# RWKV-7 mixer: the 32x32 diagonal blocks of the chunk matrices inverted column by column on VectorE

## What is computed

```python
def rwkv7_step(state, inp):
    r_t, w_t, k_t, v_t, a_t, b_t = inp
    sa = jnp.einsum('bhvk,bhk->bhv', state, a_t)
    state = (state * w_t[:, :, None, :] + sa[..., None] * b_t[:, :, None, :]
             + v_t[..., None] * k_t[:, :, None, :])
    return state, jnp.einsum('bhvk,bhk->bhv', state, r_t)
```

## Time and profile before

| what | us |
|---|---|
| median of 3 runs | 2700.04 |
| lowest and highest of them | 2699.19, 2700.79 |
| the profiled execution's own time | 2704.08 |
| its span (first to last instruction) | 2700.3 |
| busy in the span: TensorE / VectorE / ScalarE / GpSimd | 2652.0 / 2121.3 / 1292.1 / 109.4 |
| the mixer's stage from the first value product to the end of chunk 1's outputs | 803.9 to 982.0 |

### The profile page before, as it was taken

The page is one execution under the profiler, slowest core; times in us unless marked ns, Lnnn a source line. Parts: engine busy times, 40 slices in busy tenths (PEclk is TensorE's granted clock), DMA queues, the critical chain, the costliest instruction groups (busy, mean ns, idle before and its releaser), DMA issues.

```text
span 2700.3 us, 51095 instructions
## 1 busy us (share of the span) xinstructions
PE 2652.0 (98%) x20514; PEld 2458.9 (91%) x20514; DVE 2121.3 (79%) x3219; ACT 1292.1 (48%) x1780; POOL 109.4 (4%) x109
## 2 busy tenths in 40 slices
PE   8999999999999999999999999999999999999999
PEld 7998799999888989999879999986899999859999
DVE  7986589899765647995987878499878887987877
ACT  5345553443532324335565544555554464564543
POOL 0000000000013310000000000000000000000000
PEclk9999999999999999999999999999999999999999
DMA  7764267667431015764424455431345544404454
GB/s 273 280 233 157 94 258 279 238 253 280 155 140 63 1 73 219 280 233 172 157 79 156 166 185 183 168 141 63 110 156 187 188 156 155 153 19 145 168 186 155
DMA packets 61229, 456.22 MB, mean 169 GB/s; under 512 B 6840, under 2 KB 6864, under 8 KB 8736
## 3 DMA queue, kind: packets, MB, share of 16 engines
q1 hardware_dynamic: 54432, 395.86, 40.1%
q0 software_dynamic: 6656, 58.35, 5.4%
HBM read 453.12 MB, written 1.07 MB: 168 GB/s over the span
## 4 chain that ended last, share of the span: by engine, by line
PE 88%; DVE 5%; ACT 3%; DMA 3%; issue 1%; DVEq 0%; SPq 0%; ACTq 0%
PE ps L777 22%; PE ps L616 14%; PE ps L617 14%; PE ps L618 14%; PE ps L1058 3%; DMA ring<-in_weights 3%; PE ps L1452 3%; PE ps L1459 1%; ACT arena L2087 1%; PE ps L1311 1%; PE ps L1148 1%; PE ps L1141 1%; PE ps L558 1%; PE ps L1294 1%; DVE w_parts L2158 1%
## 5 line engine op out<-in xcount | busy, mean ns | idle before, releaser
L1624 ACT ACTIVATE w_parts<-ring 128x1024 fp32r<-128x1024 f32 x462 | 463.4, 1052 | 402.3 <-PE ps L616 284.9
L616 PE MATMUL ps<-normed_parts,w_parts 128*128 128x256 f32 x2160 | 602.3, 279 | 1.7 <-DVE w_parts L2158 1.7
L617 PE MATMUL ps<-normed_parts,w_parts 128*128 128x256 f32 x2160 | 603.7, 279 | 0.0
L618 PE MATMUL ps<-normed_parts,w_parts 128*128 128x256 f32 x2160 | 603.0, 279 | 0.0
L2158 DVE SCALAR_TENSOR_TENSOR w_parts<-ring,w_parts 128x1024 fp32r<-128x1024 f32 x462 | 544.6, 1220 | 50.0 <-ACT w_parts L1624 49.4
L777 PE MATMUL ps<-stream_high,half_parts 128*128 128x256 f32 x2224 | 422.8, 286 | 2.5 <-DVE half_parts L2363 1.6
L616 PEld LDWEIGHTS ps<-normed_parts,w_parts 128*128 128x128 f32 x2160 | 406.0, 188 | 2.3 <-DVE w_parts L2158 2.3
L618 PEld LDWEIGHTS ps<-normed_parts,w_parts 128*128 128x128 f32 x2160 | 406.0, 188 | 0.0
L617 PEld LDWEIGHTS ps<-normed_parts,w_parts 128*128 128x128 f32 x2160 | 405.9, 188 | 0.0
L2363 DVE SCALAR_TENSOR_TENSOR half_parts<-ring,half_parts 128x1024 fp32r<-128x1024 f32 x225 | 271.9, 1213 | 130.3 <-ACT half_parts L1711 129.4
L777 PEld LDWEIGHTS ps<-stream_high,half_parts 128*128 128x128 f32 x2224 | 347.9, 188 | 7.6 <-issue 5.6
(11 more groups left out here) (459 smaller groups left out, 4197.2 us busy)
## 6 DMA issues: line engine op xcount, KB each, us to landing
ring<-in_weights SPq DMA_DIRECT2D x374, 1024.0 KB, 4.8
arena<-in_mod_weights POOLq DMA_DIRECT2D x32, 1536.0 KB, 8.2
arena<-in_cond POOLq DMA_DIRECT2D x8, 512.0 KB, 6.6
arena<-toeplitz_rows POOLq DMA_DIRECT2D x1, 1536.0 KB, 12.3
x<-in_x SPq DMA_DIRECT2D x1, 1024.0 KB, 4.7
arena<-in_ctx POOLq DMA_DIRECT2D x1, 1024.0 KB, 5.4
out<-x SPq DMA_DIRECT2D x1, 1024.0 KB, 3.9
const<-in_const SPq DMA_DIRECT2D x1, 999.0 KB, 11.4
```

Of the source, the lines that this page charges most:

```text
L616: first = pe.matmul(into, wh, high, start=start, stop=False, skip_group_check=True)
L617: pe.matmul(into, wh, low, start=False, stop=False, skip_group_check=True)
L618: return first, pe.matmul(into, wl, high, start=False, stop=stop, skip_group_check=True)
L1624: a(w_parts[:, to, 0, cols], ring[:, at, cols], ACT.Copy).then_inc(s["w_high"], 1)
```

## The change

Levels 0 to 4, by which blocks of 32 come to be, are taken out of the doubling. In their place each of the 4 diagonal 32x32 blocks of each of the 32 matrices is inverted by itself, all 128 at once, one on each partition of VectorE. The steps are:

- TensorE multiplies `rw_b` with `AR_a` for all 16 heads of a chunk, in one group of 16 matmuls of 128 columns each (`diagonal(c)`), for both chunks ahead of the values; these are the same numbers as the first half of `products`, which are still made later.
- ScalarE keeps the diagonal blocks alone, in four copies on 32 partitions each (`keep_diagonal`), into `small_in`.
- VectorE masks them, transposes by blocks of 32 so that each partition holds one 32x32 block, sets the diagonal to 1, and runs 30 columns of elimination, each one a product and a sum of (31 - j) x j elements, each waiting for the one before. Two transposes bring the inverses back (`small_n`, `small_t`).
- `Tn` and `Tt` are set to zero beforehand, for chunk 0 by VectorE and for chunk 1 by GpSimd, and ScalarE puts the blocks in place, in eight copies on 32 partitions a chunk (`spread_small`).
- The level of n = 32 and the last one stay. GpSimd masks once for a group, with `next_t`, instead of five times.
- `narrow(5)` stands ahead of the values and its weight tile ahead of theirs in the stream. The four products of chunk 0 stand behind all values. The copies of the turned keys and b go from VectorE to ScalarE.
- The table of constants has `next_t` and `small_above` instead of `below`, `level0`, `level0_t` and `levels_t`.

The core of the diff:

```diff
-CONSTANTS = [("ident", P), ("ones", P), ("head_ones", P), ("below", P), ("upto", P), ("above", P), ("level0", P),
-             ("level0_t", P), ("levels_t", 6 * P), ("flip", P), ("head_columns", 62), ("both_rows", 16)]
+SMALL = 32
+CONSTANTS = [("ident", P), ("ones", P), ("head_ones", P), ("upto", P), ("above", P), ("next_t", P), ("flip", P),
+             ("small_above", SMALL), ("head_columns", 62), ("both_rows", 16)]
...
+    n = SMALL
+    put("next_t", ((i[:, None] // (2 * n) == i[None] // (2 * n)) & (i[None] // n % 2 == 1) & (i[:, None] // n % 2 == 0)).astype(np.float32))
+    put("small_above", (i[:, None] % n < np.arange(n)[None]).astype(np.float32))
...
+        Tn_all, Tt_all = carve(16384, 4 * NB, P), carve(18432, 4 * NB, P)
+
+        MATRICES = NT * RW_HEADS
+        small_in = carve(0, MATRICES, SMALL)
+        small_x, small_step = carve(22528, SMALL, SMALL), carve(23552, SMALL * SMALL // 4)
+        small_n, small_t = carve(0, MATRICES, SMALL), carve(1024, MATRICES, SMALL)
...
+                if c:
+                    pool.wait_ge(s["rw_u"], 2 * c)
+                    nc.gpsimd.memset(Tn_all, 0.0)
+                    nc.gpsimd.memset(Tt_all, 0.0).then_inc(s["small_zero"], 1)
+                    pool.wait_ge(s["top_C"], 6 * c)
+                for b in range(NB):
+                    pool.wait_ge(s["rwA_copied"], NB * c + b + 1)
+                    nc.gpsimd.tensor_tensor(Am[b], At[b], C("next_t").unsqueeze(1).broadcast_to((P, 4, P)), ALU.mult).then_inc(s["am_ready"], 1)
...
-                    pe.wait_ge(s["rw_r_out"], p + 1)
+                    pe.wait_ge(*((s["rw_r_out"], p + 2) if p < 3 else (s["mm_evac"], mm0 + 16)))
...
+                def diagonal(c):
+
+                    for b in range(NB):
+                        for p in in_turn:
+                            m, half = heads[b][p]
+                            bank, at = 4 + 2 * half + b // 2, (2 * (b % 2) + p % 2) * P
+                            mm = pe.matmul(ps[:, bank, at:at + P], rw_b[rows[half], m, c * P:(c + 1) * P], AR[rows[half], m, c, 0], start=True, stop=True)
+                    mm.then_inc(s["rw_side"], 1)
+
+                pe.wait_ge(s["rw_ab"], 4)
+                diagonal(0)
+                narrow(5, (P, P), free=(s["rw_r_out"], 1))
+                pe.wait_ge(s["diag_kept"], 1)
+                diagonal(1)
                 value(0)
+                value(1)
                 pe.wait_ge(s["rw_rk"], 1)
+                pe.wait_ge(s["diag_kept"], 2)
                 for p in range(4):
...
-                mm.then_inc(s["rw_bs"], 1)
-                value(1)
+                mm.then_inc(s["rw_side"], 1)
+                value(2)
...
-                mm.then_inc(s["rw_turn"], 1)
-                value(2)
+                mm.then_inc(s["rw_side"], 1)
+                value(3)
                 pe.wait_ge(s["rw_turned"], 2)
                 products(0, 0)
-                value(3)
-                products(0, 1)
                 pe.wait_ge(s["mm_evac"], mm_n[0])
...
-                mm.then_inc(s["rw_turn"], 1)
+                mm.then_inc(s["rw_side"], 1)
+                products(0, 1)
                 products(0, 2)
+                products(0, 3)
                 pe.wait_ge(s["rw_v_turned"], 1)
 
-                narrow(5, (P, P))
-                products(0, 3)
-
                 def invert(c):
 
-                    with pe.Fori(0, 4) as l:
-                        for step in ("B0", "B1", "C0", "B2", "C1", "B3", "C2", "C3"):
-                            b = int(step[1])
-                            if step[0] == "B":
-                                pe.wait_ge(s["inv_T"], 20 * c + 4 * l + b + 1)
-                                pe.wait_ge(s["am_ready"], 20 * c + 4 * l + b + 1)
...
+                    pe.wait_ge(s["small_spread"], c + 1)
                     for step in ("B0", "B1", "C0", "B2", "B3", "C1", "C2", "C3"):
                         b = int(step[1])
                         if step[0] == "B":
-                            pe.wait_ge(s["inv_T"], 20 * c + 16 + b + 1)
-                            pe.wait_ge(s["am_ready"], 20 * c + 16 + b + 1)
+                            pe.wait_ge(s["am_ready"], NB * c + b + 1)
...
+                            if b == 0:
+                                pe.wait_ge(s["rwA_copied"], NB * (c + 1))
+                                pe.wait_ge(s["rwA_masked"], 2 * NB * (c + 1))
...
+                def keep_diagonal(c):
+
+                    actv.wait_ge(s["rw_side"], c + 1)
+                    for r in small_rows:
+                        by_half = ps[r, 4:8, :].rearrange("q (h d) (e n t) -> q h (d e) n t", h=2, e=2, n=2)[:, :, :, :, r]
+                        ins = a(small_in[r, of_chunk(c), :].rearrange("q (b h n) t -> q h b n t", h=2, n=2), by_half, ACT.Copy)
+                    ins.then_inc(s["diag_kept"], 1)
+
...
+                def spread_small(c, whole, small, which):
+
+                    for r in [small_rows[i] for i in which]:
+                        ins = a(whole[r, :, r], small[r, of_chunk(c), :], ACT.Copy)
+                    return ins
...
+                keep_diagonal(0)
+                evac(g_lora[:, 0, :], ACT.Sigmoid, m=0, last=False)
+                evac(g_lora[:, 1, :], ACT.Sigmoid, m=1, incs=2)
+                keep_diagonal(1)
+                value(0, 2)
+                value(1, 2)
+                actv.wait_ge(s["rw_side"], 3)
...
+                value(2, 2)
+                actv.wait_ge(s["rw_side"], 4)
+                for i, dst in enumerate((k_tok, b_tok)):
+                    a(dst, ps[:, 4 + 2 * i:6 + 2 * i, :].rearrange("p b t -> p (b t)"), ACT.Copy).then_inc(s["rw_turned"], 1)
+                value(3, 1)
...
                 strict(0)
-                value(3)
+                actv.wait_ge(s["rw_side"], 5)
+                a(rw_v, ps[:, 0:4, :].rearrange("p (c b) t -> p c (b t)", c=NT), ACT.Copy).then_inc(s["rw_v_turned"], 1)
+                actv.wait_ge(s["small_done"], 1)
                 strict(1)
-                actv.wait_ge(s["rw_turn"], 2)
-                a(rw_v, ps[:, 0:4, :].rearrange("p (c b) t -> p c (b t)", c=NT), ACT.Copy).then_inc(s["rw_v_turned"], 1)
+                spread_small(0, Tn_all, small_n, (0, 1))
...
                 strict(2)
-                evac(g_lora[:, 0, :], ACT.Sigmoid, m=0, last=False)
-                evac(g_lora[:, 1, :], ACT.Sigmoid, m=1)
+                spread_small(0, Tn_all, small_n, (2, 3))
                 strict(3)
+                spread_small(0, Tt_all, small_t, (0, 1, 2, 3)).then_inc(s["small_spread"], 1)
...
-                    with actv.Fori(0, 4) as l:
-                        for b in range(NB):
-                            actv.wait_ge(s["inv_B"], 16 * c + 4 * l + b + 1)
-                            a(Bs[b].rearrange("p n t -> p (n t)"), ps[:, b, :], ACT.Copy).then_inc(s["inv_Bs"], 1)
...
+                actv.wait_ge(s["small_zero"], 1)
+                spread_small(1, Tn_all, small_n, (0, 1, 2, 3))
+                spread_small(1, Tt_all, small_t, (0, 1, 2, 3)).then_inc(s["small_spread"], 1)
...
-                dve.wait_ge(s["rw_turn"], 1)
-                for i, dst in enumerate((k_tok, b_tok)):
-                    nc.vector.tensor_copy(dst, ps[:, 4 + 2 * i:6 + 2 * i, :].rearrange("p b t -> p (b t)")).then_inc(s["rw_turned"], 1)
+                link.mark(nc.vector.memset(Tn_all, 0.0))
+                link.mark(nc.vector.memset(Tt_all, 0.0))
+
+                def small_inverses():
+
+                    in_turn = lambda v: v.rearrange("p h t -> p t h")
+                    mask = C("small_above", SMALL).unsqueeze(1).broadcast_to((P, MATRICES, SMALL))
+                    dve.wait_ge(s["diag_kept"], 2)
+                    link(tt(small_in, small_in, mask, ALU.mult))
+                    link(nc.vector.transpose(small_x, in_turn(small_in)))
+                    link.mark(nc.vector.memset(flat(small_x)[:, 0:SMALL * SMALL:SMALL + 1], 1.0))
+                    for j in range(1, SMALL - 1):
+                        n = SMALL - 1 - j
+                        below = small_x[:, j + 1:SMALL, 0:j]
+                        step = small_step[:, 0:n * j].rearrange("p (i k) -> p i k", i=n)
+                        link(tt(step, small_x[:, j + 1:SMALL, j:j + 1].broadcast_to((P, n, j)), small_x[:, j:j + 1, 0:j].broadcast_to((P, n, j)), ALU.mult))
+                        link(tt(below, below, step, ALU.add))
+                    nc.vector.transpose(in_turn(small_n), small_x.rearrange("p t s -> p s t"))
+                    nc.vector.transpose(in_turn(small_t), small_x).then_inc(s["small_done"], 1)
+
+                small_inverses()
...
-                    link.mark(tt(Tt[b], by[:, :, 0:P], wide("level0_t"), ALU.mult))
                     tt(Arb[c][b], by[:, :, P:S], wide("upto"), ALU.mult).then_inc(s["rwA_masked"], 1)
                     dve.wait_ge(s["rwA"], 2 * n + 2)
                     tt(Aak[b], ky[:, :, 0:P], wide("above"), ALU.mult)
...
-                    link.wait()
```

(25 more changed lines are left out.)

41 lines of the change are left out of this document (5 added, 36 removed).

## The result

The changed kernel takes **2654.39 us** (median of four runs, 2652.92 to 2655.24), the kernel before 2700.41 in the same comparison (2699.19 to 2713.57). The ratio is 0.9821 with a 95% interval of 0.9803 to 0.984: faster by 46 us, over eight times the 5.4 us that can be told from no change. The forecast was 2651.9, with a range of 2649 to 2663.

The account below looks back on a forecast made before the run. TensorE was taken as the bound (88% of the last chain), with 59.95 us of levels removed. Gains of 21.3 (chunk 0), 26.7 (chunk 1) and 0.1 (start) summed to 48.1 us, from 2700.04 to 2651.9; range 2649 to 2663.

Parts of the forecast that it names:

- Levels removed, order of TensorE, 1.9 us a diagonal block: TensorE: 59.95 us of loop levels removed over both chunks; each added block of 16 diagonal products takes 1.9 us.
- The inversion ends before the masks need VectorE: VectorE: inversion takes 26.9 us, columns 21.8 of it, done at 845.0, leaving 5.4 us of cover before the first mask.
- The page that the prediction set against its row: VectorE transposes: skill page has strided streams pay 0.7 to 1.5 extra cycles an element, some 2.4 to 5 us more.
- Past it each us of inversion goes into the sum one for one: Beyond the 5.4 us of cover, every us of VectorE's inversion lengthens the total by one us.
- GpSimd's product is clear of the chain: GpSimd's bonus product, some 5.1 us, starts at 849.4, after VectorE's inversion, so it does not stretch its operations.
- Chunk 0 gains 21.3 us: TensorE begins chunk 0's remaining step, `top_B`, at 862.5 instead of 883.78.
- Chunk 1 gains 26.7 us: TensorE begins chunk 1's `top_B` at 925.05 instead of 951.77, after eight spread copies and a 4 us gap.
- The clock in the gap, a rival at 0.08: TensorE's clock falls in the 4 us gap, 16 products cost 1.7 us more: 2653.6; chance 0.08.
- Sum: Whole kernel: 21.3 + 26.7 + 0.1 = 48.1 us gained, so 2651.9 against the median.
- Everything behind, up to the output, follows from there: Behind the two chunks' inversions, nothing changes by itself up to the output; no gain of its own was counted.
- 2.1 us at the start: TensorE's 2.08 us wait for the fourth weight tile: 0.1 us gain forecast; rival gains it all, 2649.9, chance 0.04.
- Contention, the slower rival: VectorE's 60 column operations take 1.81 us each, as beside GpSimd, 110.7 instead of 21.8 us: 2735.4; chance 0.03.

Follow-up runs that it names:

- the two runs: The changed kernel with its strided transposes, 2654.39 us, and the same kernel with all three transposes made dense, 2653.32 us.
- the two long delays: Changed kernel plus dead VectorE operations behind the columns: ten two-input ones of 1,024 columns, 2669.20 us; ten dense transposes instead, 2664.13 us.

## Why the prediction was right, and where it was not

- *Levels removed, order of TensorE, 1.9 us a diagonal block:* right. 1.98 and 1.98 from start to start in the trace.
- *The inversion ends before the masks need VectorE:* right, and it is the main step. The columns were forecast at 21.8 us and took 21.9; the fixed 0.157 us and 1.04 ns an element, from rows of other shapes, hold for chains of 30 to 240 elements. (The 0.192 in the sum is not quite 0.157 and the 0.03 read from the rows; with 0.187 it is 21.6.) Mis-sized are the three transposes, 1.96, 2.10 and 1.91 us for 1.28 and twice 1.2: 2.3 us together, so that 3.1 us of cover are left where 5.4 were forecast. The page that the prediction set against its row (the Trainium skill, "Vector Engine (DVE) Microarchitecture Reference", 5.2) was right in kind. Its table runs from about 0.65 to 1.4 extra cycles an element, which as an estimate is 2.1 to 4.4 us for the three, somewhat less than the 2.4 to 5 that the prediction gives; the measured 2.3, stride against dense in the two runs, is at the lower end. "Past it each us of inversion goes into the sum one for one" is right at the end only: the two long delays show 2.8 us more cover on TensorE's side, and a fall of the clock that takes most of it back.
- *GpSimd's product is clear of the chain:* right by 2.2 us only (chain done 848.50, product from 850.66). It took 4.54 us, not 5.1, and the two clears 1.8 each instead of 5.1; neither was in anybody's way.
- *Chunk 0 gains 21.3 us:* 20.8 (885.7 to 865.8 at the next step of the inversion, and the 0.9 by which the trace is late). The term that was mis-sized is the spread copy, 0.63 us for 0.55.
- *Chunk 1 gains 26.7 us:* 26.0 at the start of `top_B`, and 24.2 when it is done (L1164 at 953.65, now L1160 at 909.60, the 0.9, less chunk 0's 20.8). Of the 2.5 us missing, 0.6 is again the copy (eight of 0.08), and 1.8 is the clock.
- *The clock in the gap, a rival at 0.08:* it came true in every trace of the changed kernel. The argument against it was bad: one gap of 2.08 us without a fall says nothing of one twice as long. It doesn't even hold for that gap: behind the same wait at the start (1.9 to 2.2 us) the clock fell in four of the 14 traces. The fall should have stood in the sum: 1.8 us.
- *Sum:* so the mixer gave 44.9 (982.0 to 938.0 at the head sums, and the 0.9) of the 48.0 forecast. The step that is missing is that nothing behind the mixer changes ("Everything behind, up to the output, follows from there"): 3.5 us more were gained in the stretch told of above. In the profiled pair the whole is 44.9 from the mixer, less the 0.9 by which it begins later, plus 3.5, plus 0.6 from further behind, which is 48.1. The misses cancel; this is why the span fits to the tenth.
- *2.1 us at the start:* forecast 0.1 of it; TensorE still waited 1.92 us there for VectorE's part, which began at 31.69, where the prediction had it held.
- *Contention, the slower rival:* its mechanism is real, and larger than I had it (5.42 us for 1.24), but only where GpSimd works. It was argued out by time, correctly.
- *The median* is 2.5 us above the forecast, in the range. The forecast took the 48.1 from a median of 2700.04; the medians of the kernel before in the five comparisons were 2700.4 to 2703.7, so the scatter of a median is of the same size.

## What to carry to other kernels

When a chain moves to an engine that is idle at that time and is covered, its length stops mattering at once (22 us less of it gave nothing; 17.7 and 12.8 us more cost 14.8 and 9.7); what it costs is the small glue that brings its result back, on whichever engine stands right before the consumer. Put such copies into that engine's idle times before you make anything faster: here the order of sixteen copies, with some bias operations put off, was worth 9.8 us, a fifth of the change itself. And a wait that a row shows is not always a wait of that place: time gained early can shorten a wait for weights some 65 us behind it, so leave some room in the range for it.

## What the runs showed of the hardware

- A two-input VectorE operation on SBUF does not slow down beside GpSimd's two-input product but stands still until it is over: 5.42 us for 1.24 beside one of 4.54. A transpose of the same size is not touched (ten in 12.76 us).
- After a 4.53 us gap of TensorE the granted clock was at half in each of the seven traces that have one, and the next 16 products took 3.75 us for 1.95. After the 2.12 us gap ahead of chunk 0's `top_B` it fell in four of nine traces (3.38, 3.36, 3.29 and 2.54 us) and not in the others (2.02). That alone moves a run by some 1.3 us. In the kernel before, the 1.77 us gap ahead of chunk 1's levels was followed by it in one trace (a granted clock of 0.66 from 920 to 925) and not in the other.
- A copy by ScalarE on 32 partitions in pieces of 32 takes 0.63 us for 512 elements; on 128 partitions in one piece 0.55.
- GpSimd clears 2048 columns in 1.8 us, where its two-input product of as many takes 4.5.
